# Eight pieces of w_ada: weighted sums on VectorE during the first layer's merge instead of thin matmuls on TensorE

## The chip, the cores and the metric

One core of one Trainium2 chip runs the whole program. The metric is the device time of one execution in microseconds (us). All data are float32.

## The reference, cut to what matters

Two layers of an attention, gated-linear-attention and gated-unit trunk (`trunk_layer`, 256 tokens and 256 context tokens, width 1024) are followed by two layers of a second kind. The change concerns the modulation vectors of the first two layers, and where in the first layer they are made:

```python
shift, scale, gate = jnp.split(jax.nn.silu(c) @ p['w_ada'] + p['b_ada'], 3, axis=-1)
shift_c, scale_c, gate_c = jnp.split(jax.nn.silu(c_ctx) @ p['w_ada'] + p['b_ada'], 3, axis=-1)
h = x * (1.0 + scale[:, None, :]) + shift[:, None, :]
...
m = (jax.nn.sigmoid(ga) * (ya @ p['w_br_attn'])
     + jax.nn.sigmoid(gg) * (yg @ p['w_br_gla'])
     + jax.nn.sigmoid(gs) * (ys @ p['w_br_sgu']))
return m @ p['w_out']
...
x_new = layer_norm(DEEPNORM_ALPHA * x + gate[:, None, :] * out, p['post_g'], p['post_b'])
```

`w_ada` is 1024 x 3072 for each layer: six pieces of 1024 x 512 a layer, twelve in all. Each piece is multiplied by two vectors, silu(c) and silu(c_ctx), which are the two columns of `cs3`. The first four pieces (shift and scale of layer 0, `ADA_FIRST`) are wanted at once. The other eight (`ADA_LATER`: the gate of layer 0 and all of layer 1) are wanted only behind the first layer's merge.

## The kernel before, in words

Each engine runs an instruction list of its own; semaphores order them (`Ev`; `Lane.wait_ge` waits).

**Weights.** SP loads all weight pieces in the order of `PLAN` into a ring of seven units of 1 MB. A piece of 1024 x 512 takes two units, a branch piece (512 x 512) one. Each load waits until the pieces that sat in its units are done with, and SP issues in order, so a load that waits holds back all behind it. `piece_done` says which event frees a piece.

**First layer, woven part** (41 to 395 us). TensorE, VectorE, ScalarE and GpSimd each run three generators, `dense`, `attention` and `gla`, one step at a time in an order written out by hand, `ORDER_A[0]`. Between the dense steps stand the eight later pieces of w_ada: a product step `ef` (`ada_products`: eight thin matmuls, each with two columns of `cs3` as the stationary side and 512 columns of weights as the moving side, and with its result at one of four row offsets of the bank), a copy on ScalarE (`ada_rows`), four transposes (`ada_columns`, `es`) and a short sum on VectorE (`ada_sum`).

**Merge of the first layer** (395 to 596 us). TensorE does the branch product of piece a0 (four groups of 128x512), then five pieces in the order g0, s0, a1, g1, s1 (`LATER`). Each of those has a gate part "m" and a branch part "b", and each part is made of seven half-size products (`WINOGRAD`, in the order 1, 2, 6, 7, 5, 4, 3). Products 6, 5 and 3 go to the bank of product 1, and 4 to that of 7, so each waits for ScalarE's copy of what the bank held. VectorE makes the sums over inputs (`input_sums`), adds the parts (`put`) and applies the gates (`gated`), in `later_piece`; GpSimd makes the sums over weights (`weight_sums`: four of 128x1024 for an "m" part, four of 128x512 for a "b" part) and adds the branches (four of 128x512 for each piece but a1). `gated` of pieces g and s writes the scratch tile `TM`, so each waits for GpSimd's add of the one before. After the merge come the gate rows (`gb`) and the product with w_out (`ou`).

Of the kernel before, what the change touches and what calls it, by code (L numbers as in the profile page):

```python
# [9 lines left out]
ALU = mybir.AluOpType  # L10
# [40 lines left out]
    "daadddddaddaddddadadgaaadgadgaadgdgaagdagadagadgadagadgagadgaadgadaaggadaaaggadggaadggagadgagdgaaddgaggadgggaa"  # L51
    "dgagdagdagdggadgdgaadgaagadagaagdadgaadgadagddaadaaaddaaadaagagadgaaaggagadgagagagadgadaggdaggggg",
# [9 lines left out]
def plan_a(l):  # L62
# [3 lines left out]
    if l == 0:  # L66
        for n, (m, j) in enumerate(ADA_LATER):
            out.insert(2 * n + 1, (f"a{m}ada{j}", 4096))
# [25 lines left out]
def dense_a(l):  # L94
# [3 lines left out]
    nth = [0]  # L98

    def ada():  # L100
        k = nth[0]
        nth[0] += 1
        if l:
            return []
        return ([("es", k - 1, "V")] if k else []) + ([("ef", k, "A")] if k < len(ADA_LATER) else [])

    q = [[("q", t, "A")] for t in tiles]
    kv = [[("kv", t, "A")] for t in range(4)]
    if l == 0:
        steps = q + [ada()] + kv + [[("lr", 0, "A")] + ada(), []]  # L110
    else:
        steps = kv[:2] + [[("hx", 0, "-")]] + kv[2:] + [[("lr", 0, "A")] + ada(), []] + q + [ada()]
    for name, kind in (("gqk", "A"), ("gv", "A"), ("ag", "T"), ("gg", "T"), ("su", "A"), ("sg", "T")):
        steps += [[(name, c, kind)] for c in range(4)] + [ada()]
    steps += [[("row", 0, "V")], [("bt", 0, "A")], [("sv", tiles[0], "A")], [("sv", tiles[1], "A")]]
    for t in tiles:
# [4 lines left out]
        else:  # L121
            steps += [[("mx", t, "V")] + ada()]
# [71 lines left out]
def build_program(nc, wf, consts, cT, xin, xinT, pa, ra, rpost, pb, rfin, out):  # L194
    with ExitStack() as ctx:
# [54 lines left out]
        par = ma.take(PA_SW)  # L250
        row = ma.take(640)
# [35 lines left out]
        HS = {n: r3(mw.take(1024), 4) for n in "1234"}  # L287
        E7 = SIGS.rearrange("p (a g n) -> p a g n", a=2, g=2)
# [83 lines left out]
        mg_sum = ev("mg_sum", 54)  # L372
        MS_T, MS_11, MS_22, MS_21, MS_B = 4, 8, 9, 10, 11
# [5 lines left out]
        FLAT[0] = FIRST + FLAT[0]  # L379
# [42 lines left out]
        MG_1, MG_11, MG_6, MG_7, MG_5, MG_22, MG_21, MG_12, MG_B = range(9)  # L422
# [60 lines left out]
        MGI = [{g: i for i, g in enumerate(x)} for x in MG]  # L483
        GATE = {g: i for i, g in enumerate(x for x in MG[1] if x[0] == "m")}
# [10 lines left out]
        for l in range(2):  # L495
# [3 lines left out]
            for i, g in enumerate(g for g in FLAT[l] if g[2] != "-" and (l, g[0]) != (0, "q")):  # L499
# [30 lines left out]
            seq = []  # L530
            for g in MG[l]:
                if l and g[0] == "m":
# [11 lines left out]
                seq.append((("mg", l) + g, freed))  # L544
            seq += [(("gb", l, i), gb_act.at(l, i)) for i in range(gb_pe.per[l])]
# [74 lines left out]
        def piece_done():  # L620
# [3 lines left out]
            for n, (l, j) in enumerate(ADA_LATER):  # L624
                out[f"a{l}ada{j}"] = dense_done(0, "ef", n)
# [56 lines left out]
        def merge_start(l):  # L682

            return [at_y.end(l), gl_y.end(l), gl_ms.end(l), gl_rs.end(l), dn_act.end(l), dn_dve.end(l), ys_done.end(l)]
# [67 lines left out]
        def _(e):  # L752
# [41 lines left out]
            def ada_columns(n, g, first):  # L794
                p.wait_ge(landed(d_id), dense_act(0, first, n))
                b = bank("dense", 0, g, n)
                for i in range(4):
                    ins = transpose(b, i, PT4[n % 2][:, 128 * i:128 * i + 128])
# [24 lines left out]
            def dense(l):  # L823
                L0 = l0(l)
                for step in DENSE[l]:
                    for n, i, kind in step:
                        if n == "ef":
                            ada_products(i, "ef", *ADA_LATER[i])
                            continue
                        if n == "es":  # L830
                            ada_columns(i, "es", "ef")
                            continue
# [189 lines left out]
            def layer_a(l):  # L1022
                L0 = l0(l)
                if l == 0:
                    for n in range(2):
                        ada_products(n, "pf", *ADA_FIRST[n])
                    for n in range(2):
                        ada_columns(n, "ps", "pf")
# [5 lines left out]
                    ada_columns(2, "ps", "pf")  # L1034
# [1654 lines left out]
```

## Time and profile before

| | |
|---|---|
| time, median of 3 runs | 1562.16 us (1559.05 to 1563.88) |
| the profiled execution: its own time | 1564.0 us |
| its span, first to last instruction | 1562.2 us |
| mean granted TensorE clock | 0.995 |

Read the shares of the engines first, then the chain that ended last, then the stages one by one: an engine's share of the whole span hides that the stages have different limits.

### The profile page before, as it was taken

Reading aid. Unit: us, or ns where it says so; the run is one execution under the profiler, and the core shown is the slowest. Engines: PE = TensorE matmul, PEld = TensorE weight load, DVE = VectorE, ACT = ScalarE, POOL = GpSimd, SP = SyncE. Lnnn points to the kernel's source line nnn. Section 1 sums busy time; section 2 is a strip of 40 time slices with the busy share of each in tenths; the row PEclk is TensorE's granted clock in tenths of the full one; section 3 lists DMA queues with packets and bytes.
Section 4 is the critical chain, followed back from the end, with each engine's and each line's share of the span. In section 5 each row is a group of like instructions: output and inputs, shape, how many; then the busy total and the mean of one; then the engine's idle time right before and its main releaser. Section 6 shows DMA issues by size and latency. Waiting matters only on the chain.

```text
span 1562.2 us, 19171 instructions
## 1 busy us (share of the span) xinstructions
PE 1516.4 (97%) x7888; PEld 1077.2 (69%) x7888; DVE 681.1 (44%) x1460; ACT 415.0 (27%) x814; POOL 281.9 (18%) x314
## 2 busy tenths in 40 slices
PE   6999999999999999999999999999999999999997
PEld 2544544455688885555877888588888758888873
DVE  1233433464633343523344311365687216568721
ACT  1122325232312210121235320134233213423320
POOL 0322210131455441113002102110100011010010
PEclk9999999999999999999999999999999999999999
DMA  8642222300122231322322243423221323332231
GB/s 362 262 175 108 108 108 108 135 27 17 65 81 81 97 123 68 150 108 97 119 108 108 102 156 120 175 102 144 109 110 71 147 115 149 126 112 106 88 128 40
DMA packets 17370, 184.22 MB, mean 118 GB/s; under 512 B 2306, under 2 KB 2818, under 8 KB 4740
## 3 DMA queue, kind: packets, MB, share of 16 engines
q1 hardware_dynamic: 17284, 183.01, 30.7%
q8 instruction: 62, 1.02, 0.3%
q14 instruction: 24, 0.20, 0.0%
HBM read 181.95 MB, written 1.05 MB: 117 GB/s over the span
## 4 chain that ended last, share of the span: by engine, by line
PE 89%; ACT 3%; DVE 3%; issue 2%; DMA 1%; POOL 1%; SPq 0%; POOLq 0%; ACTq 0%; DVEq 0%
PE ps L756 86%; PE ps L811 3%; DVE arena L1749 1%; DVE arena L1755 1%; DMA arena<-in_wf 1%; POOL arena L2362 1%; ACT arena L1333 1%; ACT L1709 0%; ACT L1707 0%; DVE arena L1752 0%; ACT arena L1577 0%; ACT arena L1707 0%; ACT arena L1593 0%; ACT L1595 0%; ACT L1593 0%
## 5 line engine op out<-in xcount | busy, mean ns | idle before, releaser
L756 PE MATMUL ps<-arena 128*128 128x256 f32 (+7 forms) x7396 | 1467.1, 383 | 33.8 <-DMA arena<-in_wf 12.3
L756 PEld LDWEIGHTS ps<-arena 128*128 128x128 f32 (+5 forms) x7396 | 1023.6, 178 | 445.4 <-issue 311.9
L2362 POOL TENSOR_TENSOR arena<-arena 128x256 f32<-128x256 f32 (+6 forms) x254 | 247.3, 994 | 825.8 <-DVE arena L1755 409.3
L1755 DVE SCALAR_TENSOR_TENSOR arena<-arena 128x256 f32<-128x256 f32 (+4 forms) x470 | 231.0, 545 | 143.4 <-ACT arena L1475 38.8
L1333 ACT ACTIVATE arena<-ps 128x512 f32<-128x512 f32 (+2 forms) x280 | 134.9, 505 | 448.3 <-PE ps L756 370.5
L1749 DVE TENSOR_TENSOR arena<-arena 128x512 f32<-128x512 f32 (+14 forms) x190 | 140.4, 761 | 170.9 <-ACT arena L1333 95.8
L1755 DVE SCALAR_TENSOR_TENSOR arena<-arena,ps 128x256 f32<-128x256 f32 (+2 forms) x121 | 54.0, 456 | 207.2 <-PE ps L756 96.9
L1749 DVE TENSOR_TENSOR arena<-ps,arena 128x512 f32<-128x512 f32 (+16 forms) x120 | 48.8, 434 | 106.0 <-PE ps L756 97.3
L811 PEld LDWEIGHTS ps<-arena 128*128 128x128 f32 x488 | 55.7, 141 | 29.4 <-issue 19.5
L811 PE MATMUL ps<-arena 128*128 128x128 f32 x488 | 71.5, 278 | 3.1 <-ACT arena L1611 1.5
L1752 DVE TENSOR_SCALAR arena<-arena 128x256 f32<-128x256 f32 (+9 forms) x181 | 62.8, 382 | 15.7 <-POOL arena L2362 10.8
L2366 POOL TENSOR_SCALAR arena<-arena 128x1 f32<-128x1 f32 (+2 forms) x22 | 16.2, 737 | 222.3 <-DVE arena L1802 79.2
L1755 DVE SCALAR_TENSOR_TENSOR arena<-ps,arena 128x128 f32<-128x128 f32 (+2 forms) x84 | 30.0, 407 | 59.3 <-PE ps L756 59.2
L1934 DVE COPY_PREDICATED arena<-arena,ps 128x512 f32<-128x512 uint32 (+1 forms) x56 | 30.1, 591 | 46.5 <-PE ps L756 46.5
L1559 ACT ACTIVATE arena<-ps,arena 128x256 f32<-128x256 f32 x32 | 14.9, 473 | 112.6 <-PE ps L756 107.3
L1372 ACT ACTIVATE arena<-ps 128x512 f32<-128x512 f32 (+1 forms) x24 | 11.8, 490 | 103.7 <-PE ps L756 103.7
L2535 POOL TENSOR_SCALAR arena<-arena 128x128 f32<-128x128 f32 x16 | 11.3, 726 | 110.7 <-DVE arena L1755 110.7
L1863 DVE TENSOR_REDUCE arena<-ps 128x1 f32<-128x512 f32 (+1 forms) x48 | 26.4, 590 | 9.6 <-PE ps L756 9.6
L1412 ACT ACTIVATE arena<-ps,arena 128x512 f32<-128x512 f32 (+1 forms) x48 | 29.0, 615 | 4.4 <-DVE arena L1752 4.4
L1381 ACT ACTIVATE arena<-ps 128x256 f32<-128x256 f32 (+1 forms) x24 | 10.1, 419 | 73.3 <-PE ps L756 73.3
L1455 ACT ACTIVATE arena<-arena 128x1024 f32<-128x1024 f32 (+1 forms) x28 | 23.3, 838 | 2.5 <-POOL arena L2362 2.5
L1563 ACT ACTIVATE arena<-ps 128x256 f32<-128x256 f32 x24 | 9.1, 380 | 54.7 <-PE ps L756 54.7
(96 smaller groups left out, 294.4 us busy)
## 6 DMA issues: line engine op xcount, KB each, us to landing
arena<-in_wf SPq DMA_DIRECT2D x69, 2048.0 KB, 8.3
arena<-in_wf SPq DMA_DIRECT2D x22, 1024.0 KB, 6.5
arena<-in_wf SPq DMA_DIRECT2D x2, 1152.0 KB, 7.7
arena<-in_xinT SPq DMA_DIRECT2D x2, 1024.0 KB, 15.9
arena<-in_xin SPq DMA_DIRECT2D x4, 512.0 KB, 3.9
arena<-in_rp SPq DMA_DIRECT2D x2, 1024.0 KB, 8.2
arena<-in_consts SPq DMA_DIRECT2D x1, 1410.0 KB, 21.6
arena<-in_pa SPq DMA_DIRECT2D x2, 532.0 KB, 9.4
```

Of the source, the lines that this page charges most:

```text
L756: return e.matmul(o, l, r, start=start, stop=stop, skip_group_check=True)
L811: return e.transpose(b[:, 128 * i:128 * i + rows], x, ident[0:rows, 0:rows])
L1333: return e.activation(o, i, ACT.Copy, **kw)
L1412: e.activation(Pb[h][:, 0:L], psum("att", l, "s", 2 * w + h)[:, 0:L], ACT.Exp, bias=sm[:, 1, h:h + 1], scale=0.125, accum_out=sm[:, 2, h:h ...
L1455: e.activation(x, x, ACT.Exp, scale=1.0 / 16).then_inc(gl_fe.hit(l, 7 * hp + n), 1)
L1749: return e.tensor_tensor(o, x, y, op)
L1752: return e.tensor_scalar(o, x, s1, None, op0) if s2 is None else e.tensor_scalar(o, x, s1, s2, op0, op1)
L1755: return e.scalar_tensor_tensor(out=o, in0=x, scalar=s, in1=y, op0=op0, op1=op1)
L1863: ins = e.reduce_max(sm[:, 0, h:h + 1], psum("att", l, "s", 2 * w + h)[:, 0:L], AX)
L1934: e.copy_predicated(att[:, tl[0]:4, h, :], both(2 ** n).unsqueeze(1).to_broadcast([128, nt, 128]), r3(psum("gla", l, "l", k)[:, L0:512], n ...
L2362: return e.tensor_tensor(o, x, y, op)
L2366: e.tensor_scalar(o, x, eps, None, ALU.add).then_inc(g.own(), 1)
```

## The change

The eight later pieces leave the woven part. Each is now made in the merge: VectorE adds up, over the eight chunks of 128 rows, weights times one number for each partition, once for silu(c) and once for silu(c_ctx): 16 instructions of 128x512 for a piece (`ada_later`). They are issued in quarters of four instructions, at places in the merge's VectorE list. TensorE then turns both sums (`et` and `es`, four transposes each) behind named products of the merge, and VectorE reduces them (`ada_turned`). `ORDER_A[0]` is a new string; the pieces stand elsewhere in the ring's order; ScalarE's tanh of the first quarter gate comes behind two copies instead of ahead of them.

```diff
+    if l == 0:
+        for (m, j), before in zip(ADA_LATER, ("ba0", "bg0", "ms0", "bs0", "ba1", "mg1", "bg1", "bs1")):
+            out.insert([n for n, _ in out].index("a0" + before), (f"a{m}ada{j}", 4096))
...
+        ACC = [[par_row[:, 0:512], par_row[:, 512:1024]], [par_row[:, 1024:1536], qkv_gv[:, 4608:5120]]]
+        BEHIND = [(*LATER[n], kind, x) for n, kind, x in ((0, "m", 7), (0, "b", 7), (1, "m", 5), (2, "m", 6), (2, "b", 7),
+                                                          (3, "m", 5), (4, "m", 6), (4, "b", 7))]
...
-                out[f"a{l}ada{j}"] = dense_done(0, "ef", n)
+                out[f"a{l}ada{j}"] = ada_acc.at(0, n)
...
 TensorE, behind each product of the merge
+                    for n, k, _ in turned_after(l, g):
+                        ada_columns(k, n, ACC[k % 2][n == "et"], ada_acc.at(0, k))
-                p.wait_ge(dense_dve(0, "es", 7))
+                p.wait_ge(dense_dve(0, "et", 7))
...
 ScalarE
-                    a.wait_ge(mg_dve.at(0, branch(*(LATER[n - 1] if n else ("a", 0)), 3)))
+                    a.wait_ge(mg_dve.at(0, branch(*LATER[n - 1], 3)) if n else None)
...
 VectorE
+            def ada_later():
+                for k, (l, j) in enumerate(ADA_LATER):
+                    w = weights(f"a{l}ada{j}", 8)
+                    made = [None, None]
+                    for kk in range(8):
+                        v.wait_ge(pieces[f"a{l}ada{j}"][2], dense_done(0, "et", k - 2) if k > 1 else None)
+                        for r in range(2):
+                            acc = ACC[k % 2][r]
+                            if kk == 0:
+                                ins = ts(acc, w[:, kk, :], cs3[:, kk, r:r + 1], None, ALU.mult)
+                            else:
+                                v.wait_ge(made[r])
+                                ins = stt(acc, w[:, kk, :], cs3[:, kk, r:r + 1], acc, ALU.mult, ALU.add)
...
+                        if kk % 2:
+                            yield
...
+                if n:
+                    next(quarters, None)
                 for kind, dst, o in (("m", SIG4, 0), ("b", BR, MS_B - MS_11)):
...
                     put(kind, 2, dst, 1, 1, MS_11 + o)
+                    if not o:
+                        turned("11")
+                        next(quarters, None)
+                        next(quarters, None)
...
                     tt(result(dst, 2, 2), E7, result(dst, 2, 2), ALU.add)
+                    if not o:
+                        turned("22")
+                        next(quarters, None)
                     if o:
                         gated(1, 2, 2, result(BR, 2, 2), mg_sum.at(0, 10 * n + MS_B + 1))
+                        turned("b22")
                     put(kind, 7, dst, 2, 1, MS_21 + o)
+                    if not o:
+                        next(quarters, None)
+                        next(quarters, None)
...
 VectorE, behind each of the four gate products of piece a0
+                            if l == 0:
+                                next(quarters)
```

The pieces are numbered k = 0 to 7 below; k is turned behind m7 of g0, b7 of g0, m5 of s0, m6 of a1, b7 of a1, m5 of g1, m6 of s1 and b7 of s1.

## Rows read from the trace of the kernel before

**Rows 1.** The page: shares of the engines, and the chain by engine.
```profile
PE 1516.4 (97%) x7888; PEld 1077.2 (69%) x7888; DVE 681.1 (44%) x1460; ACT 415.0 (27%) x814; POOL 281.9 (18%) x314
...
PE 89%; ACT 3%; DVE 3%; issue 2%; DMA 1%; POOL 1%; SPq 0%; POOLq 0%; ACTq 0%; DVEq 0%
```

**Rows 2.** Stages: length, busy us (count) of PE, PEld, DVE, ACT, POOL, granted clock.
```profile
41.00:395.00 354.00, 351.74 (x1519) 177.29 (x1520) 143.29 (x276) 110.14 (x216) 67.43 (x85) 1.00 0.31 120
...
402.40:424.30 21.90, 20.45 (x79) 14.56 (x77) 20.64 (x13) 1.76 (x4) 19.37 (x8) 1.00 0.00 1
424.30:446.80 22.50, 22.49 (x104) 19.85 (x105) 5.13 (x7) 5.28 (x9) 9.24 (x5) 1.00 0.25 94
446.80:591.90 145.10, 145.10 (x675) 127.78 (x673) 57.66 (x56) 28.71 (x48) 72.44 (x42) 1.00 0.24 88
```

**Rows 3.** Timeline of TensorE in short windows: dense products, thin products, transposes.
```profile
86.61 10.46 PE L756 MATMUL ps<-arena 128*128 128x512 f32 x24
...
106.04 1.90 PE L756 MATMUL ps<-arena 128*2 128x512 f32 x16
...
122.34 0.60 PE L811 MATMUL ps<-arena 128*128 128x128 f32 x4
```

**Rows 4.** Timeline of TensorE through the merge: start, length, count, idle before.
```profile
416.71 7.17 PE L756 MATMUL ps<-arena 128*128 128x256 f32 x32 [1.03 <-ACT arena L1333]
424.31 167.75 PE L756 MATMUL ps<-arena 128*128 128x256 f32 x776 [0.42 <-ACT arena L1333]
591.90 1.91 PE L811 MATMUL ps<-arena 128*128 128x128 f32 x16
596.34 56.78 PE L756 MATMUL ps<-arena 128*128 128x512 f32 x128 [2.53 <-issue]
```

**Rows 5.** Timeline of VectorE: start of the merge, end of g0, start of s0.
```profile
402.39 11.09 DVE L1749 TENSOR_TENSOR arena<-arena 128x1024 f32<-128x1024 f32 x4
413.40 2.47 DVE L1755 SCALAR_TENSOR_TENSOR arena<-arena,ps 128x512 f32<-128x512 f32 x4
...
447.10 2.82 DVE L1755 SCALAR_TENSOR_TENSOR arena<-arena 128x512 f32<-128x512 f32 x1 [0.78 <-POOL arena L2362]
451.31 0.69 DVE L1755 SCALAR_TENSOR_TENSOR arena<-arena,ps 128x512 f32<-128x512 f32 x1 [1.38 <-POOL arena L2362]
451.91 5.71 DVE L1749 TENSOR_TENSOR arena<-arena 128x512 f32<-128x512 f32 x4
457.54 0.68 DVE L1749 TENSOR_TENSOR arena<-ps,arena 128x512 f32<-128x512 f32 x1
```

**Rows 6.** Timeline of GpSimd in the same stretch.
```profile
402.43 19.53 POOL L2362 TENSOR_TENSOR arena<-arena 128x1024 f32<-128x1024 f32 x8 [39.27 <-DVE arena L1755]
...
445.80 3.58 POOL L2362 TENSOR_TENSOR arena<-arena 128x512 f32<-128x512 f32 x2 [1.85 <-DVE arena L1755]
...
452.07 8.03 POOL L2362 TENSOR_TENSOR arena<-arena 128x512 f32<-128x512 f32 x5 [0.80 <-DVE arena L1755]
471.34 4.67 POOL L2362 TENSOR_TENSOR arena<-arena 128x1024 f32<-128x1024 f32 x2 [11.24 <-PE ps L756]
```

**Rows 7.** Timeline of VectorE in the third layer: a chain of weighted sums.
```profile
1060.27 3.25 DVE L1755 SCALAR_TENSOR_TENSOR arena<-arena 128x256 f32<-128x256 f32 x8
```

**Rows 8.** Groups of VectorE by shape, whole span: count, busy us, mean ns.
```profile
L1752 DVE TENSOR_SCALAR arena<-arena 128x512 f32<-128x512 f32 x40 | 20.5, 545 | 11.3 <-POOL arena L2362 10.8
...
L1863 DVE TENSOR_REDUCE arena<-ps 128x1 f32<-128x512 f32 x32 | 20.4, 678 | 5.7 <-PE ps L756 5.7
```

**Rows 9.** The same view in steps of 1 us, behind TensorE's wait before w_out.
```profile
598.00:599.00 1.00, 1.00 (x2) 0.34 (x1) 0.00 (x0) 0.00 (x0) 0.00 (x0) 0.50 0.79 242
599.00:600.00 1.00, 1.00 (x3) 0.53 (x2) 0.00 (x0) 0.00 (x0) 0.00 (x0) 0.70 1.00 328
```

**Rows 10.** DMA issues of weights: KB each, median us from issue to landing.
```profile
arena<-in_wf SPq DMA_DIRECT2D x69, 2048.0 KB, 8.3
arena<-in_wf SPq DMA_DIRECT2D x22, 1024.0 KB, 6.5
```

More of the change, by code:

```diff
@@ L249, in build_program @@
         GK, GQ = GKQ[:, :, 0, :], GKQ[:, :, 1, :]
-        par = ma.take(PA_SW)
-        row = ma.take(640)
+        par_row = ma.take(PA_SW + 640)
+        par, row = par_row[:, 0:PA_SW], par_row[:, PA_SW:PA_SW + 640]
         tv = ma.take(2048)
@@ L378, in build_program @@
                  ("ps", 2, "V"), ("qh", 3, "-"), ("ps", 3, "V")]
-        FLAT[0] = FIRST + FLAT[0]
+        TURNED = [("e" + "st"[r], k, "V") for k in range(8) for r in range(2)]
+        FLAT[0] = FIRST + FLAT[0] + TURNED
         GROUP = [{g[:2]: i for i, g in enumerate(f)} for f in FLAT]
@@ L498, in build_program @@
                     hold(("ht", s, kp), 3 + i % 5, (ht_dve if s else ht_act).at(1, 2 * kp + 1))
-            for i, g in enumerate(g for g in FLAT[l] if g[2] != "-" and (l, g[0]) != (0, "q")):
+            for i, g in enumerate(g for g in FLAT[l] if g[2] != "-" and (l, g[0]) != (0, "q") and g not in TURNED):
                 hold(("dense", l) + g[:2], i % 2, (dense_act if g[2] == "A" else dense_dve)(l, *g[:2]))
@@ L529, in build_program @@
                 hold(("gla", l, n, k), 5 + i % 3, by.at(l, k))
-            seq = []
+            seq, extra = [], []
             for g in MG[l]:
+                seq += extra
+                extra = [(("dense", 0, n, k), dense_dve(0, n, k)) for n, k, _ in turned_after(l, g)]
                 if l and g[0] == "m":
@@ L1766, in ada_sum, with ada_turned @@
                     ).then_inc(dn_dve.hit(0, BY_DVE[0][(g, n)]), 1)
+            def ada_later():
[11 more added lines that the diff above has]
+                                ins = stt(acc, w[:, kk, :], cs3[:, kk, r:r + 1], acc, ALU.mult, ALU.add)
+                            if (kk, r) == (7, 1):
+                                ins.then_inc(ada_acc.hit(0, k), 1)
+                            else:
+                                ins.then_inc(v.own(), 1)
+                                made[r] = v.now()
+                        if kk % 2:
+                            yield
+            def ada_turned(k):
+                l, j = ADA_LATER[k]
+                for r, g in enumerate(("es", "et")):
+                    v.wait_ge(dense_done(0, g, k), landed(d_bada, l))
+                    a4 = AS[:, 4 * r:4 * r + 4]
+                    e.tensor_reduce(a4, r3(psum("dense", 0, g, k), 4), AX, ALU.add).then_inc(v.own(), 1)
+                    v.wait_ge(v.now())
+                    stt(r3(SCOL[l], 24)[:, 4 * j:4 * j + 4, r], a4, 1.0 if j in (2, 3) else 0.0,
+                        BADA[:, 24 * l + 4 * j:24 * l + 4 * j + 4], ALU.add, ALU.add
+                        ).then_inc(dn_dve.hit(0, BY_DVE[0][(g, k)]), 1)
+                    v.wait_ge(dense_dve(0, g, k))
             def dense(l):
@@ L1984, in later_piece, with turned @@
                 input_sums(HB, {"a": AG, "g": GG, "s": SG}[br], 10 * n + MS_T)
+                def turned(place):
+                    for k, at in enumerate(((0, "22"), (0, "b22"), (1, "22"), (2, "22"), (2, "b22"), (3, "22"), (4, "22"),
+                                            (4, "b22"))):
+                        if at == (n, place):
+                            ada_turned(k)
+                if n:
+                    next(quarters, None)
                 for kind, dst, o in (("m", SIG4, 0), ("b", BR, MS_B - MS_11)):
@@ L2019, in layer_a @@
                     input_sums(HS, hT, 0)
+                    quarters = ada_later()
                 for j in range(2):
```

87 lines of the change are left out of this document (35 added, 52 removed).

## The prediction

> **What bounds the kernel now.** The page comes first: TensorE is busy for 97% of the span, and the chain that ended last is TensorE for 89% [rows 1]. So a change pays only as far as it takes time from TensorE's list, and costs as far as it makes TensorE wait. The windows by stage say where there is room: in the woven part TensorE is busy 351.7 of 354.0 us, in the last four merge pieces 145.1 of 145.1, while VectorE is busy 57.7 of those 145.1 [rows 2]. The timeline of TensorE shows the merge's waits: 1.0 and 0.4 us in piece g0, 2.5 us ahead of w_out, nothing between [rows 4]. VectorE's and GpSimd's timelines show what the shares hide: how long their instructions take when both run [rows 5, 6].
>
> **What the woven part gives back.** A thin product is 16 records of TensorE. Dense records of 512 columns come every 0.43 us (24 in 10.46), but the 16 thin ones take 1.90 together, since they run beside one another [rows 3]. I count 1.8 for a piece, the last record's tail lying under the next product: 8 x 1.8 = 14.4 us, not 8 x 6.9 = 55. Four transposes pass in 0.60 with their tail, 16 in 1.91 [rows 3, 4]: 0.11 each, 0.44 a piece, 3.5 for eight. Removed: 17.9 us. ScalarE's copies and VectorE's small sums go too; both engines are mostly idle there (110 and 143 of 354 busy [rows 2]), so they count nothing. The new order string keeps TensorE's other work. It could at best remove the 2.3 us of idle time, and could bring waits, since 17.9 us of filler are gone between the same chains; I count 0, and 0 to +5 for the range. In it the last GLA product stands alone behind the last dense group, not in a pair, so I let VectorE enter the merge 5.3 us behind TensorE's first merge product. Before it was 7.4: that product began at 395.0 (416.7 less the 1.0 wait, less 32 records at 0.43 and 32 at 0.216), and VectorE began at 402.4 [rows 4, 5].
>
> **What the merge takes on, without waits.** TensorE: 8 x 2 x 4 = 64 transposes at 0.11 = +7.0. VectorE: 16 multiplies at 0.5 [rows 8] and 112 weighted sums. A chain of weighted sums of 128x512 is not in the trace. Four independent ones with one input from PSUM take 2.47, 0.61 apart, and one alone lasts 0.69 [rows 5]; in the chain of 256 columns eight take 3.25, 0.40 apart [rows 7], so chained ones follow each other almost, but not quite, end to end, which for 512 columns I put at 0.67. Bounds 0.61 and 0.67; I take the middle, 0.64. That is 72 + 8 = 80 us, and 16 reductions at 0.68 with a small sum each, 0.9 in all, make 14. VectorE's idle time in the merge is 1.3 + 17.4 + 87.4 = 106 us [rows 2]. So 94 of 106 us would be filled before any wait is counted.
>
> **What they wait for.** With GpSimd working, VectorE's instructions with two SBUF inputs stretch: four of 128x1024 take 11.09 us beside GpSimd's sums, four of 128x512 take 5.71 though one takes 0.69 alone, and one gate takes 2.82 while GpSimd finishes a sum; the one that reads PSUM keeps its 0.68 [rows 5, 6]. GpSimd stretches too (4.67 for two of 1024 alone, 19.53 for four of 1024 and four of 512 beside VectorE; 8.03 for five of 512 against 1.27 for one). The numbers fit turns taken one whole instruction at a time: 1.15 + 2.2 us for a pair of 1024, 0.6 + 1.15 for a pair of 512. All 128 new instructions are of the kind that waits. A rule of the Trainium skill says the same (SBUF — State Buffer, section Who interferes with whom): a VectorE instruction with two SBUF inputs and a GpSimd one that reads SBUF exclude each other for the whole instruction. By that rule the idle 106 us aren't free for sums, and it speaks against the change. The trace agrees with it (5.71 against 4 x 0.6).
>
> **The wait that TensorE gets.** Each turning stands in TensorE's list and waits for its accumulation; all products behind it wait too. I walked the merge, instruction by instruction, with those durations, with turns between VectorE and GpSimd, and 8.3 and 6.5 us for a load [rows 10]. The same walk of the kernel before puts the start of w_out 201.4 us behind the first merge product; the rows have 596.3 - 395.0 = 201.3 [rows 4]. One step in full, piece s0, from TensorE's first product on: the gates of g0 end 6 us in (446.8 against 452.0 now [rows 5], and a turning more), input sums with GpSimd beside 5.7, a quarter 2.7, `put` 0.7, two quarters 5.3, and about 2 more for the rest of GpSimd's sums: 22 to 23. TensorE has its five "m" products done at 5 x 3.45 = 17.3. So it waits 5 to 6 us for k = 2. Likewise, each at 0.61 and at 0.67 a sum:
> - k = 0, behind m7 of g0: 2.5 and 3.4 (VectorE does 11.1 us of input sums, four gates and 16 sums, TensorE needs 27.6);
> - b6 of g0: 3.3 and 4.5. It needs ScalarE's copy of b1, in whose list the tanh of a `put` stands, and that `put` now has three quarters and a reduction ahead of it;
> - m6 of s0: 2.5 and 3.5 (ScalarE's first copy waits for the last gate of g0);
> - k = 2: 5.3 and 6.0; k = 5, behind m5 of g1: 3.9 and 4.6;
> - k = 3 and k = 6, behind m6 of a1 and s1: 2.0 and 2.3 each. There only the input sums and one quarter fit in 10.4 us, of which 5 are gone with the gates before;
> - m6 of a1, g1, s1: 1.5 and 2.7 together.
>
> Sum 23.0 and 29.3; middle 26.2. The two waits in g0 now go in it (in the walk 2.5 us with their like), because ScalarE no longer waits for VectorE there: -2.5. Ahead of w_out the wait grows by 1.3, as the last reduction (1.8) stands before three gates. So the merge: 7.0 + 26.2 - 2.5 + 1.3 = +32.0, 28.9 and 34.9 at the bounds.
>
> The ring: bg0 sits where piece 0 sat, so its load waits for the accumulation, 6.5 us before GpSimd's next sums; ba1 and bs1 wait for k = 3 and 6 alike, mg1 and ms1 for the piece before and k = 5. In the walk each lands before TensorE needs it, and what is late is GpSimd, whose sums fall onto VectorE's quarters; that is in the sum. Behind the merge, w_out's second half waits for k = 7 and lands about when it is needed: 0, and 3 for the range.
>
> TensorE's clock: behind the 2.5 us wait it runs at half speed to about 599.6, some 3.3 us, a loss of 1.7 [rows 9]. Five of the waits are as long. But TensorE then waits for VectorE again, which was not slowed, so most of it is swallowed: I count 0, and up to 5 x 1.7 = 8.5 for the range.
>
> **The sum.** -17.9 + 32.0 = +14.1 us. On the profiled span 1562.2 that is 1576.3, its own time 1564.0 giving 1578.1; on the median 1562.16, 1576.3. Bounds of this case: 28.9 - 17.9 = +11 and 34.9 - 17.9 + 5 + 3 + 4 = +29, thus 1573 to 1591.
>
> **The rivals.**
> - *The sums fit in* (faster). VectorE and GpSimd hardly meet, and TensorE sees only its own list: -17.9 + 7.0 - 2.5 + 1.3 and the one wait that a walk without turns leaves (2.2, m6 of s0) = -9.9, 1552. For it: 106 us of idle time for 94 us of work. Against it: the 5.71 and 2.82 rows, and in piece a1 even that idle time lies behind the product that waits. It decides at the sum of waits: below 17.9 - 7.0 + 2.5 - 1.3 = 12 us the change pays. Chance 0.17.
> - *Half the waits* (about the same). If the quarters mostly slip past GpSimd, the waits at k = 2, 3, 5, 6 that a chain without turns still has, 1 to 4 us each, leave some 12 us: +0, 1562. Chance 0.11.
> - *VectorE and GpSimd bound the merge* (slower still). If a sum costs 0.8 us, the walk gives waits of 43 us and +49 for the merge, +31 with the woven part: 1593; clock losses that aren't swallowed lead to the same place. For it: turns cost more than a pair's sum in the first rows (3.3 us a pair of 1024). Chance 0.14.
> - My forecast: 0.58.
>
> **Range and chances.** The likeliest case has 1573 to 1591. The range that leaves out no more than 2 in 10 takes in the faster side too: 1551 to 1592. A measurement of this kernel tells about 0.3% (5 us) from no change. Faster by more than that: 0.18 (the first rival and a bit of the second); within: 0.11; slower: 0.71.
>
> **What would show it.** In the woven part TensorE's busy time falls by 18 us, and by its other waits it is seen whether the new order holds. In the merge, VectorE's weighted sums show single durations well over 0.69 where GpSimd runs; TensorE's waits are released by VectorE ahead of transposes (k = 2, 5, 3, 6, in that order of length) and by ScalarE ahead of b6 of g0; the granted clock drops behind them. VectorE is busy for over 85% of the merge. The prediction is wrong if the weighted sums keep 0.6 us beside GpSimd, if a sum costs nearer 0.4, or if VectorE is far enough ahead that TensorE finds each accumulation done.

## Result: 1578.1 us, and the profile after

The changed kernel takes 1578.08 us (median, 1576.53 to 1581.74) beside 1561.66 of the kernel before on the same chip (1559.05 to 1563.88): ratio 1.0109, 95% interval [1.0085, 1.0133]. It is slower. Predicted were 1576.3, in 1551 to 1592, with 0.71 for slower. The profiled execution has 1581.74 as its own time, the longest of the four, and a span of 1579.9.

The page after, shares and chain [rows 1 before]:

```profile
PE 1514.2 (96%) x7792; PEld 1081.3 (68%) x7792; DVE 789.9 (50%) x1604; ACT 410.1 (26%) x806; POOL 285.2 (18%) x314
...
PE 60%; DVE 8%; ACT 3%; issue 2%; POOL 2%; DMA 0%; POOLq 0%; ACTq 0%; DVEq 0%
```

TensorE's busy time hardly moved, 1516.4 to 1514.2. VectorE has 109 us more, and its share of the chain went from 3% to 8%. The page alone says "still TensorE": the changed kernel's chain has 60% of TensorE where it had 89%. The windows say where it broke (length, busy of PE, PEld, DVE, ACT, POOL, then the clock; the woven part, the merge up to w_out, the rest) [rows 2]:

```profile
41.00:373.60 332.60, 332.40 (x1359) 171.24 (x1360) 141.77 (x262) 108.58 (x210) 66.20 (x85) 1.00 0.20 75
373.60:611.90 238.30, 212.99 (x953) 177.56 (x951) 198.04 (x240) 40.20 (x67) 108.22 (x56) 0.97 0.36 140
611.90:1579.90 968.00, 941.39 (x5370) 723.28 (x5370) 444.81 (x1084) 255.66 (x520) 109.33 (x168) 0.99 0.31 115
```

The first merge product starts at 373.65 (the row that holds it ends at 401.25; less 32 records at 0.43 and 64 at 0.216). Before it was 395.0, so the woven part gave back **21.35 us**. The product with w_out starts at 611.95, before at 596.34: the merge takes 238.3 for 201.3, **+37.0 us**. Together +15.6 at w_out.

In the timelines below, L762 is TensorE's products, L817 its transposes, L1753 VectorE's weighted sums and gates, L1747 its sums of two tensors, L1750 its multiplies, L2416 GpSimd's sums and L1335 ScalarE's copies. TensorE through the merge: start, length, count, idle before and its releaser [rows 4]:

```profile
403.09 1.09 PE L817 MATMUL ps<-arena 128*128 128x128 f32 x8 [1.84 <-DVE arena L1753]
422.37 6.59 PE L762 MATMUL ps<-arena 128*128 128x256 f32 x16 [4.38 <-ACT arena L1335]
443.25 10.63 PE L762 MATMUL ps<-arena 128*128 128x256 f32 x48 [1.32 <-ACT arena L1335]
458.83 1.91 PE L817 MATMUL ps<-arena 128*128 128x128 f32 x8 [4.96 <-DVE arena L1753]
488.29 3.72 PE L762 MATMUL ps<-arena 128*128 128x256 f32 x16 [0.79 <-ACT arena L1335]
493.79 1.10 PE L817 MATMUL ps<-arena 128*128 128x128 f32 x8 [1.78 <-DVE arena L1753]
530.18 10.63 PE L762 MATMUL ps<-arena 128*128 128x256 f32 x48 [1.61 <-ACT arena L1335]
543.13 1.09 PE L817 MATMUL ps<-arena 128*128 128x128 f32 x8 [2.33 <-DVE arena L1753]
572.60 3.72 PE L762 MATMUL ps<-arena 128*128 128x256 f32 x16 [0.79 <-ACT arena L1335]
578.11 1.09 PE L817 MATMUL ps<-arena 128*128 128x128 f32 x8 [1.78 <-DVE arena L1753]
607.03 1.52 PE L817 MATMUL ps<-arena 128*128 128x128 f32 x12 [1.05 <-DVE arena L1753]
610.61 0.65 PE L817 MATMUL ps<-arena 128*128 128x128 f32 x4 [2.06 <-DVE arena L1753]
611.95 8.40 PE L762 MATMUL ps<-arena 128*128 128x512 f32 x15 [0.69 <-POOL arena L2416]
```

Each x8 row of transposes (L817) with a wait is one turned piece: k = 0, 2, 3, 5, 6. Each L762 row that waits for ScalarE's copy (L1335) is a product 6. The waits ahead of w_out's rows belong to the last piece. Look at 458.83: the same eight transposes that take 1.09 elsewhere take 1.91 behind the longest wait. The windows of 2 us there give the reason, the granted clock (last but two):

```profile
458.00:460.00 2.00, 1.17 (x6) 1.17 (x7) 1.46 (x4) 0.59 (x1) 0.00 (x0) 0.73 0.50 90
460.00:462.00 2.00, 2.00 (x8) 1.73 (x7) 1.86 (x5) 0.04 (x1) 0.00 (x0) 0.50 0.64 229
462.00:464.00 2.00, 2.00 (x10) 1.73 (x9) 1.97 (x4) 0.00 (x0) 0.00 (x0) 0.91 0.98 418
```

After 4.96 us without work the clock is at 0.50, the level of 1.2 GHz, to about 462.

VectorE's timeline shows what its sums cost, alone and beside GpSimd [rows 5]:

```profile
393.81 2.73 DVE L1753 SCALAR_TENSOR_TENSOR arena<-arena 128x512 f32<-128x512 f32 x4
...
406.87 8.11 DVE L1753 SCALAR_TENSOR_TENSOR arena<-arena 128x512 f32<-128x512 f32 x6
...
416.22 0.16 DVE L1753 SCALAR_TENSOR_TENSOR arena<-arena 128x4 f32<-128x4 f32 x1
...
437.42 1.55 DVE L1753 SCALAR_TENSOR_TENSOR arena<-arena 128x4 f32<-128x4 f32 x1
...
442.48 5.72 DVE L1747 TENSOR_TENSOR arena<-arena 128x512 f32<-128x512 f32 x4
448.12 4.76 DVE L1753 SCALAR_TENSOR_TENSOR arena<-arena 128x512 f32<-128x512 f32 x4
...
453.40 5.38 DVE L1753 SCALAR_TENSOR_TENSOR arena<-arena 128x512 f32<-128x512 f32 x8
...
465.70 9.58 DVE L1753 SCALAR_TENSOR_TENSOR arena<-arena 128x512 f32<-128x512 f32 x8
```

GpSimd's timeline in the same stretch [rows 6]:

```profile
407.92 6.52 POOL L2416 TENSOR_TENSOR arena<-arena 128x512 f32<-128x512 f32 x4 [16.64 <-DMA arena<-in_wf]
...
442.64 8.36 POOL L2416 TENSOR_TENSOR arena<-arena 128x512 f32<-128x512 f32 x5 [0.80 <-DVE arena L1753]
468.65 5.41 POOL L2416 TENSOR_TENSOR arena<-arena 128x1024 f32<-128x1024 f32 x2 [17.65 <-PE ps L762]
```

Between 451.0 and 468.6 GpSimd is still, and eight sums take 5.38, 0.66 apart. Across GpSimd's pairs eight take 9.58, and six take 8.11. The 4-column sum (0.16) becomes 1.55: it starts at 437.42, in the middle of a GpSimd sum of 128x1024 that runs from 436.60 to 438.95, and ends at 438.97. The chain of 512 columns that the trace of before didn't have is thus 2.73 for four, 0.66 apart: the upper of my two bounds.

The rest is not the change's. Behind the start of w_out the profiled execution takes 968.0, before 965.9, and in the runs below, whose code from there on is the same but for the PSUM banks in three of them, 960.8 to 965.9. I put the 2 us down to the scatter of one profile.

### The profile page after: what moved, and what is told of

The parts are those of the page before. It is cut to its first block, busy times and chain, and to the rows that moved or that the text cites. A ratio compares the mean times of both kernels' runs of the same rounds, so it can differ in the third digit from the quotient of the medians.

```text
span 1579.9 us, 19120 instructions
## 1 busy us (share of the span) xinstructions
PE 1514.2 (96%) x7792; PEld 1081.3 (68%) x7792; DVE 789.9 (50%) x1604; ACT 410.1 (26%) x806; POOL 285.2 (18%) x314
## 3 DMA queue, kind: packets, MB, share of 16 engines
HBM read 181.95 MB, written 1.05 MB: 116 GB/s over the span
## 4 chain that ended last, share of the span: by engine, by line
PE 60%; DVE 8%; ACT 3%; issue 2%; POOL 2%; DMA 0%; POOLq 0%; ACTq 0%; DVEq 0%
PE ps L762 58%; DVE arena L1753 5%; DVE arena L1747 3%; PE ps L817 2%; POOL arena L2416 2%; ACT arena L1335 1%; DVE arena L1750 0%; ACT L1707 0%; ACT L1705 0%; DMA arena<-in_wf 0%; DVE arena L1792 0%; ACT arena L1575 0%; ACT arena L1705 0%; ACT arena L1591 0%; ACT L1593 0%
## 5 line engine op out<-in xcount | busy, mean ns | idle before, releaser
L762 PE MATMUL ps<-arena 128*128 128x256 f32 (+10 forms) x7268 | 1461.6, 382 | 37.6 <-ACT arena L1335 12.0
L762 PEld LDWEIGHTS ps<-arena 128*128 128x128 f32 (+5 forms) x7268 | 1023.0, 180 | 438.9 <-issue 296.8
L1753 DVE SCALAR_TENSOR_TENSOR arena<-arena 128x256 f32<-128x256 f32 (+4 forms) x590 | 333.3, 619 | 153.6 <-ACT arena L1473 46.1
L2416 POOL TENSOR_TENSOR arena<-arena 128x256 f32<-128x256 f32 (+6 forms) x254 | 250.6, 1008 | 851.5 <-DVE arena L1753 412.6
L1335 ACT ACTIVATE arena<-ps 128x512 f32<-128x512 f32 (+3 forms) x272 | 130.1, 502 | 470.6 <-PE ps L762 396.3
L1747 DVE TENSOR_TENSOR arena<-arena 128x512 f32<-128x512 f32 (+14 forms) x190 | 131.5, 715 | 120.3 <-ACT arena L1335 42.9
L1753 DVE SCALAR_TENSOR_TENSOR arena<-arena,ps 128x256 f32<-128x256 f32 (+2 forms) x121 | 54.3, 456 | 204.2 <-PE ps L762 98.4
L817 PE MATMUL ps<-arena 128*128 128x128 f32 x520 | 76.9, 280 | 18.2 <-DVE arena L1753 15.8
L817 PEld LDWEIGHTS ps<-arena 128*128 128x128 f32 x520 | 60.5, 142 | 48.7 <-issue 21.6
L1747 DVE TENSOR_TENSOR arena<-ps,arena 128x512 f32<-128x512 f32 (+16 forms) x120 | 48.6, 434 | 67.6 <-PE ps L762 58.8
L1750 DVE TENSOR_SCALAR arena<-arena 128x256 f32<-128x256 f32 (+8 forms) x197 | 71.4, 398 | 15.8 <-POOL arena L2416 10.8
L1753 DVE SCALAR_TENSOR_TENSOR arena<-ps,arena 128x128 f32<-128x128 f32 (+2 forms) x84 | 30.1, 407 | 69.3 <-PE ps L762 69.2
```

Of the source, the lines that this page charges most:

```text
L762: return e.matmul(o, l, r, start=start, stop=stop, skip_group_check=True)
L817: return e.transpose(b[:, 128 * i:128 * i + rows], x, ident[0:rows, 0:rows])
L1335: return e.activation(o, i, ACT.Copy, **kw)
L1747: return e.tensor_tensor(o, x, y, op)
L1750: return e.tensor_scalar(o, x, s1, None, op0) if s2 is None else e.tensor_scalar(o, x, s1, s2, op0, op1)
L1753: return e.scalar_tensor_tensor(out=o, in0=x, scalar=s, in1=y, op0=op0, op1=op1)
```

## The experiments

All are made from the changed kernel unless it is said. "Merge" is from the first merge product to w_out's start in each profile. The last transposes of the woven part stand at 363.30 in the changed kernel, 10.35 ahead of the first merge product; I take the same 10.35 in each run. "Walk" is what the hand walk gives for that kernel, as in the expectations. They take 0.66 us for a sum, so the changed kernel's walk is 235 and not the 233.3 (201.3 + 32.0) of the prediction. The 209 of "PSUM, second places" counts lost clock too; the 234 below it doesn't and stands beside 207.

| run | median us (before beside it) | ratio, 95% | merge | walk |
|---|---|---|---|---|
| the kernel before | | | 201.3 | 201.4 |
| the changed kernel | 1578.08 (1561.66) | 1.0109 [1.0085, 1.0133] | 238.3 | 235 |
| small weight sums | 1548.93 (1561.08) | 0.992 [0.9898, 0.9941] | 208.1 | 208 |
| running sums in PSUM | 1568.76 (1561.08) | 1.0051 [1.0033, 1.0069] | 231.3 | 223 |
| other places | 1558.6 (1561.08) | 0.9989 [0.9976, 1.0003] | 221.8 | 217 |
| PSUM and places | 1556.11 (1561.08) | 0.9966 [0.9953, 0.9979] | 219.6 | 211 |
| few sums | 1558.38 (1561.27) | 0.9983 [0.9971, 0.9996] | 219.1 | 212 |
| resident data | 1588.72 (1561.27) | 1.0184 [1.0167, 1.0201] | 252.2 | 243 |
| left out | 1540.16 (1561.27) | 0.9866 [0.9851, 0.988] | 199.4 | |
| sums in the woven part | 1606.64 (1561.27) | 1.0299 [1.0281, 1.0317] | | |
| PSUM, second places | **1545.54** (1558.84) | **0.9912** [0.9899, 0.9926] | 208.8 | 209 |
| second places, SBUF | 1571.71 (1559.68) | 1.0073 [1.0056, 1.009] | 233.0 | 234 |
| before, ScalarE's order | 1557.84 (1558.84) | 0.9988 [0.9979, 0.9997] | | |

**Take GpSimd's share away.** The theory was turns between VectorE and GpSimd; the rival, a chain of sums too long by itself.

```diff
-                    w11, w12, w21, w22 = (quarter(w, k, f) for f, k in ("11", "12", "21", "22"))
+                    w11, w12, w21, w22 = (quarter(w, k, f)[:, :, 0:16] for f, k in ("11", "12", "21", "22"))
+                    o = {x: y[:, :, 0:16] for x, y in o.items()}
```

> The changed kernel, with GpSimd's weight sums of the five later pieces cut to 16 of their 256 columns (the rest of WS and WB keeps old numbers); everything waits for everything as before, and VectorE's 128 new instructions stay. Theory of turns (VectorE's sums with two SBUF inputs and GpSimd's sums take turns): nearly all waits go, w_out starts about 27 us earlier in the merge, 1548 to 1553 us, VectorE's sums come 0.66 us apart nearly everywhere and their mean falls from 0.94 to about 0.70 us. Rival, the chain of sums alone is too long for the places where it is turned: VectorE's sums were the bound by their number, so the time stays within 5 us of 1578. Rival, GpSimd late with the weight sums themselves: also faster, but VectorE's mean of a sum would not fall.

1548.9, within the range on record. The changed kernel's merge stands 31.9 us above 199.4 + 7.0 (the merge without the pieces, from the run that leaves them out, and the 64 transposes); here 30.2 of them go, though VectorE has all its sums. VectorE's group of sums in that merge (count, busy, mean ns):

```profile
L1753 DVE SCALAR_TENSOR_TENSOR arena<-arena 128x512 f32<-128x512 f32 x129 | 88.3, 738 | 6.1 <-ACT arena L1473 3.3 <-POOL arena L2416 1.6
```

In the changed kernel the same 129 have a mean of 940 ns. The rival falls: the number of sums isn't what TensorE waits for. The second rival, GpSimd late by itself, asked for a mean that doesn't fall; as GpSimd is also done sooner here, it is the PSUM pair below that leaves its work as it was.

**Take VectorE's share away.**

```diff
+                            if (kk, r) not in ((0, 0), (7, 1)):
+                                continue
-                            if kk == 0:
+                            if (kk, r) in ((0, 0), (7, 1)):
```

> The changed kernel with 14 of the 16 sum instructions of each piece left out (one chunk's product stands for the sum of eight); loads, turnings, reductions, places and GpSimd's sums stay. Theory of turns: the waits come from the product of the two engines' work, so taking VectorE's share away gives as much as taking GpSimd's did: by the walk 212 us from the first merge product to w_out for 235, thus 1555, 1551 to 1559. Rival, the turnings and the small sums behind them cost, wherever VectorE stands: 1565 or more.

1558.4, within the range on record but 3 us over its centre. One wait of 6.1 us is new: ScalarE's first copy of s0 waits for the last gate of g0, and GpSimd's wide sums, which had waited 17.7 us for a load, fell on just those gates (one gate waits 3.5 us and lasts 2.8). Each engine's share taken away gives 20 to 29 us, which together is more than the 31.9 there are: the cost is in their meeting. The rival asked for 1565 or more.

**Is it the ring?** The sums read hT, which is in SBUF, and the pieces aren't loaded.

```diff
-        for (m, j), before in zip(ADA_LATER, ("ba0", "bg0", "ms0", "bs0", "ba1", "mg1", "bg1", "bs1")):
-            out.insert([n for n, _ in out].index("a0" + before), (f"a{m}ada{j}", 4096))
...
-                    w = weights(f"a{l}ada{j}", 8)
+                    w = hT
```

> The changed kernel, but the sums read the layer's input hT, which lies in SBUF, with a constant as the factor; the eight pieces are not loaded at all and hold nothing of the ring. Same instructions, same places. Theory of turns: loads don't set the waits, the time stays at 1578, or grows by up to 8 us, since GpSimd's weight sums then come earlier and fall on the a0 stage's first sums. Rival, the ring (pieces that sit in it until their sums are done hold back the loads of the branch pieces, GpSimd starts late): the time falls by 5 us or more, to 1573 or less.

1588.7, over 10 us slower (8 at most were expected), so the range on record was missed; the rival asked for a gain. A freer ring makes it worse: GpSimd's first sums, which had waited 16.6 us for a load between the wide and the narrow ones, now follow without a break, and VectorE's first sums of a quarter stretch (two multiplies 3.39 for 2.38, the two sums behind them 3.42 for 1.40):

```profile
377.76 19.44 POOL L2413 TENSOR_TENSOR arena<-arena 128x1024 f32<-128x1024 f32 x8 [43.93 <-DVE arena L1750]
```

The first turning then waits 5.3 us for 1.8. More of the loss comes later: k = 3 and k = 6 wait 5.94 us each, where the changed kernel waits 1.78. GpSimd's narrow sums for a1 follow there at once (five instructions from 487.14 on, 8.34 us), where they had waited 9.26 us for a load, and the input sums beside them take 5.71 for 3.56. The late loads were a help.

**Leave the pieces out,** loads, sums, turnings and all (a constant stands for their vectors).

> The changed kernel without the eight later pieces: no load, sum, turning or reduction of them (the vectors they make are a constant). It shows the two halves of the sum apart: the woven part as changed, and the merge without its new work. From the changed kernel's trace the woven part gave back 21 us, and ScalarE's new order should save the 2.5 us of waits in piece g0: 1562 - 21 - 2.5 = 1538, 1534 to 1542. If the woven part's 21 us came from the ring rather than from TensorE's list, the trace shows it by a shorter woven part still (over 1 us less than in the changed kernel). Rival, ScalarE's order gives nothing: the merge up to w_out stays at 201 us.

1540.2, and w_out's product starts at

```profile
573.03 55.17 PE L747 MATMUL ps<-arena 128*128 128x512 f32 x128 [2.54 <-issue]
```

The woven part ends where it ended in the changed kernel, so its 21.35 us don't hang on the loads of the pieces. The merge takes 199.4, 1.9 less than before: that is ScalarE's order. In one sum: what the change moved to the merge costs 238.3 - 199.4 = 38.9 us there.

**ScalarE's order alone,** in the kernel before.

```diff
-        MG_1, MG_11, MG_6, MG_7, MG_5, MG_22, MG_21, MG_12, MG_B = range(9)
+        MG_1, MG_6, MG_7, MG_11, MG_5, MG_22, MG_21, MG_12, MG_B = range(9)
```

> The kernel before with only ScalarE's part of the change: the tanh of the first quarter gate behind the copies of products 6 and 7, and the wait for piece a0's last gate moved to the copies that write its tile. The two waits of TensorE in piece g0 (1.0 and 0.4 us) go, and the time with them: 1560, 1558 to 1562. Rival, nothing: 1561 to 1562, the waits stay or others take their place. In neither case does it explain more than 2.5 of the change's microseconds.

w_out's product starts at 594.00 for 596.34, the two waits in g0 are gone, and 1557.84 stands beside 1558.84, 0.1% less, with an interval that just leaves out no change: 0.5 to 3 us. The change's effect is of that size or nearly: the expectation named 2.5 as the most.

**The running sum in PSUM.** A weighted sum then has one SBUF input; the last writes SBUF.

```diff
+                hold(("acc", r), 6 + r, ada_acc.at(0, 7))
...
-                            acc = ACC[k % 2][r]
+                            acc, o = psum("acc", r), ACC[k % 2][r] if kk == 7 else psum("acc", r)
```

> The changed kernel, the two running sums of a piece kept in two PSUM banks (only the last of the eight sums writes SBUF), so that each weighted sum has one SBUF input and one from PSUM; the merge's other banks rotate over six instead of eight. Same places, same work. Theory of turns, in which an instruction with one SBUF input doesn't take turns with GpSimd: sums keep 0.66 us beside GpSimd, and by the walk of the merge with these numbers 12 us go: 1566, 1561 to 1570. Rival, the chain's length and not the turns: 1578 or, as a bank's rotation is tighter, slower. Rival, any SBUF input takes turns: unchanged within 3 us.

**Other places** for quarters, turnings and loads, same instructions.

> The changed kernel, same instructions, other places: most turnings stand later in TensorE's list and the quarters of sums stand where the walk of the merge finds the fewest waits (three quarters ahead of the input sums of pieces a1 and g1, none in the a0 stage but two), the pieces of w_ada one or two places earlier in the ring. Theory of turns by the walk: 217 us from the first merge product to w_out instead of 235, thus 1560, 1556 to 1568. Rival, VectorE and GpSimd are already the bound of the merge (their busy time and turns fill it): places can't help, 1573 to 1582.

**Both,** with places of its own:

> Running sums in PSUM and places chosen for that case. Theory of turns by the walk: 211 us from the first merge product to w_out, thus 1554, 1549 to 1560; if the sums don't take turns and nothing else comes in, it beats the kernel before (1562). Rival, the chain's length or the tighter rotation of banks: 1565 or more.

1568.8, 1558.6 and 1556.1, all in their ranges. "Any SBUF input takes turns" and "VectorE and GpSimd are the bound, places can't help" both fall: places alone give 20 us. The last is the first version with all of its work that is faster than the kernel before. Both PSUM runs stood 8 to 9 us above their walk in the merge. In the first of them the two longest waits of TensorE are these:

```profile
439.39 15.70 PE L764 MATMUL ps<-arena 128*128 128x256 f32 x64 [4.61 <-DVE arena L1755]
522.53 16.78 PE L764 MATMUL ps<-arena 128*128 128x256 f32 x64 [5.09 <-DVE arena L1755]
```

They stand ahead of m2 of s0 and of g1. With a rotation over six banks m2 takes the bank of product b1 of the piece before, which the last gate frees; with eight it takes one that has long been free. The changed kernel waits 1.32 and 1.61 us there, one product later. Without the bank wait m6 could start 0.69 us behind the last gate, as it does there; with it m2 starts at the gate's end and takes 3.45 first. So I estimate that the tighter rotation, which the expectation named in a rival, took back 2 x 2.8 = 5.6 us of what PSUM gave at these places. I had put the 8 to 9 us down to two other things that the walk lacked: the 128x4 sums, which take turns too (0.16 or 1.55, above), and lost clock, and chose the places anew with both in the walk ("p" and "s" are ahead of and behind a piece's input sums, "11" to "b22" the places behind its `put` and gate steps):

```diff
-        BEHIND = [(*LATER[n], kind, x) for n, kind, x in ((0, "m", 7), (0, "b", 7), (1, "m", 5), (2, "m", 6), (2, "b", 7),
-                                                          (3, "m", 5), (4, "m", 6), (4, "b", 7))]
+        BEHIND = [(*LATER[n], kind, x) for n, kind, x in (
+            (0, "m", 7), (1, "m", 3), (2, "m", 2), (2, "b", 1), (3, "m", 2), (4, "m", 2), (4, "m", 3), (4, "b", 6))]
...
+            QUARTERS = [{'21': 2, 's': 1, '22': 1},
+                        {'11': 3, 'b11': 1, 'b22': 1},
+                        {'11': 2, 'p': 1, '21': 2, '22': 1},
+                        {'21': 1, 'p': 5, 'b22': 1, '22': 1},
+                        {'11': 4, '22': 1}]
...
+                    for k, at in enumerate(((0, "b11"), (1, "21"), (2, "p"), (2, "b11"), (3, "b11"), (4, "21"), (4, "b11"), (4, "b11"))):
...
+                            for _ in range((1, 2, 1, 0)[c] if l == 0 else 0):
```

> As the run with running sums in PSUM and chosen places, the places chosen anew after that run: the walk now also counts 1.5 us of lost clock for each wait over 1.9 us and 0.68 to 0.70 us for the first multiply into PSUM, and finds 209 us from the first merge product to w_out (the run before measured 219.7 where the same walk gives 214 and one clock loss more). Theory of turns: 1549, 1546 to 1554, three waits of TensorE at most that are over 1 us. Rival, the 5 to 6 us by which both PSUM runs were above their walk come from the tighter banks or from PSUM itself: 1553 to 1557, no better than before.

1545.5, 0.9912 [0.9899, 0.9926]: **faster than both kernels,** by 13 us and by some 31 (0.9912 to 1.0109), and 0.5 us below its range of 1546 to 1554. The merge takes 208.8, 2.4 above the 199.4 + 7.0 of one in which TensorE waits for nothing new. Its window:

```profile
373.60:582.20 208.60, 204.94 (x952) 173.88 (x951) 174.68 (x240) 39.75 (x66) 98.34 (x56) 1.00 0.42 159
```

**The same places, the sum in SBUF.** Two kernels that differ in where the running sum lies, in what that brings with it (six banks or eight), and in the place of one wait of VectorE's for `et`, which ends no wait of its sums in either trace.

> The places of the fastest run (the second set, 1545.5), but the running sums in SBUF as in the changed kernel, eight banks again. The two differ only in where the running sum lies. Theory of turns: by the walk 234 us from the first merge product to w_out against 207, six waits of TensorE over 2 us come back, 1545.5 + 26 = 1572, 1566 to 1578. Rival, the gain of that run came from its places and not from PSUM: 1545 to 1555.

1571.7, where 1572 was expected. Each works alone, places by 20 us and PSUM by 9 against the changed kernel, but neither alone is clearly faster than the kernel before (0.9989 and 1.0051); these places, made for PSUM, cost 26 us with the sums in SBUF. The same stretch of the two, VectorE and GpSimd, first with PSUM:

```profile
390.58 5.35 DVE L1755 SCALAR_TENSOR_TENSOR ps<-arena,ps 128x512 f32<-128x512 f32 x8
...
392.11 5.08 POOL L2423 TENSOR_TENSOR arena<-arena 128x512 f32<-128x512 f32 x4 [0.61 <-DMA arena<-in_wf]
```

and with SBUF:

```profile
388.07 4.47 DVE L1750 TENSOR_SCALAR arena<-arena 128x512 f32<-128x512 f32 x2
...
395.40 7.82 DVE L1753 SCALAR_TENSOR_TENSOR arena<-arena 128x512 f32<-128x512 f32 x8
...
392.79 6.59 POOL L2420 TENSOR_TENSOR arena<-arena 128x512 f32<-128x512 f32 x4 [0.52 <-DMA arena<-in_wf]
```

With PSUM eight sums run from 390.58 to 395.93, beside GpSimd's from 392.11 on, and both keep their pace: 0.66 and 1.27 apiece. With SBUF both stretch, and two multiplies take 4.47. The waits come back to TensorE, five of over 2 us where six were expected. Three of them:

```profile
406.53 1.97 PE L817 MATMUL ps<-arena 128*128 128x128 f32 x8 [4.77 <-DVE arena L1753]
...
523.46 1.97 PE L817 MATMUL ps<-arena 128*128 128x128 f32 x8 [4.07 <-DVE arena L1753]
...
567.07 17.53 PE L762 MATMUL ps<-arena 128*128 128x256 f32 x80 [2.99 <-ACT arena L1335]
```

The Trainium skill (SBUF — State Buffer, section Who interferes with whom) states the other half of the rule that the prediction cited: a VectorE instruction with at most one SBUF input, outside the two-port modes, doesn't contend with GpSimd. The 5.35 and 5.08 agree. The condition may matter here: the multiplies have one SBUF input as well, and from SBUF to SBUF two of them take 4.47 beside GpSimd's wide sums, where into PSUM two take 1.40 (at 387.36 in the fastest run, GpSimd's wide sums running to 391.49). In which mode they ran no trace shows.

**A place where GpSimd is idle,** the woven part, in the order string of the kernel before: a miss.

```diff
+    for k in range(0 if l else 8):
+        steps[(9, 13, 18, 23, 28, 33, 38, 43)[k]].insert(0, ("es", k, "V"))
+        steps[(11, 15, 20, 25, 30, 35, 40, 46)[k]].insert(0, ("et", k, "V"))
+        for i in ((4, 5, 6, 7), (8, 9, 10, 11), (13, 14, 15, 16), ..., (38, 39, 40, 41))[k]:
+            steps[i].append(("eq", k, "-"))
```

> The same sums on VectorE, turned and reduced in the same way, but in the woven part in the order string of the kernel before, not in the merge: quarters behind the dense steps of the first layer, the turnings of a piece one dense piece later, running sums in four tiles that are free there. GpSimd is busy 67 us of 354 there, not 104 of 201. Theory of turns (the place is what costs): thin products gone 14.4, 32 transposes more +3.5, ScalarE's order in the merge -2.5, so 1562 - 13 = 1549, 1544 to 1556. Rival, a quarter of 2.7 us on VectorE delays the attention's and the gated-linear chain's own steps wherever it stands: TensorE waits in the woven part, 1562 or more.

1606.6, where 1549 was expected: the slowest of all, and the rival's case. The last transposes of the woven part stand at 427.62, before at 387.31, 40.3 us later; the merge is 2.0 us shorter. TensorE's waits from 41 to 410 us: total, times, longest:

```profile
PE ps L812 <- DVE arena L1751: 10.0, 2, 9.4
PE ps L757 <- DVE arena L1751: 5.7, 2, 3.3
PE ps L757 <- DVE arena L1968: 5.5, 2, 2.9
PE ps L812 <- DVE arena L1745: 3.9, 2, 3.0
PE ps L757 <- DMA arena<-in_wf: 3.7, 1, 3.7
```

The first turning comes 9.4 us too early, the dense piece behind waits 3.7 for its load, and the gated-linear chain's own VectorE steps (L1968) are late behind quarters. The granted clock is 0.94 over the stretch from 41 to 411. "Idle" in a window of 354 us was no room: VectorE's steps there lie inside chains that TensorE follows closely. How much of it better places would save, I haven't tried.

## Why the prediction was right

The forecast's case came, and for its reason: TensorE waits for sums that take turns with GpSimd, at the places that the walk had named. The total is nearer than its parts, and that is luck. Forecast were -17.9 + 32.0 = +14.1 us, measured up to w_out -21.35 + 37.0 = +15.6. The merge lies above its own 28.9 to 34.9 (the terms as printed add up to 28.8 and 35.1); slower matmuls, counted as 0, cost 9 us more, while the waits came out 4.6 and the woven part 3.45 below the forecast. Point by point, by its steps:

- **Woven part, -17.9: measured -21.35.** Thin products and transposes came out 1.4 us too small (busy 351.74 to 332.40 is 19.3), and "new order 0" was 2.1 too low: the 2.3 us of idle time fell to 0.2. That is what I allowed the order at best; whether it is the order's doing or that of the steps gone was not tested apart.
- **Transposes 7.0:** eight take 1.04 to 1.10 with their tail, less what overlaps; right as far as the rows tell.
- **Waits, 26.2: measured 21.6** (the first ten of the timeline), below the range of 23.0 to 29.3. The list held, in the order k = 2, 5, then 3 and 6: k0 1.8 (2.5 to 3.4), b6 of g0 4.4 (3.3 to 4.5), m6 of s0 1.3 (2.5 to 3.5), k2 5.0 (5.3 to 6.0), k3 and k6 1.8 each (2.0 to 2.3), k5 2.3 (3.9 to 4.6), m6 of a1, g1, s1 3.2 together (1.5 to 2.7). VectorE's input sums began 4.3 us behind the first merge product (377.98), not 5.3, which helped k0.
- **Ahead of w_out +1.3:** 1.05 + 2.06 + 0.69 for 2.53, +1.3. **ScalarE's order -2.5:** -1.9.
- **The clock, 0 with up to 8.5: the mis-sized term.** 238.3 less 199.4, 7.0 and the waits beyond those that the kernel without the pieces has (25.4 - 2.5) leaves 9.1 us. It can be read another way: TensorE is busy 213.0 us in the merge, before 197.4 and 7.0 are due for transposes, so 8.6 more for the same work. In the run with second places in SBUF the same sum leaves 9.1 again (waits 20.0), in the fastest run, with one wait over 2 us, 1.3. Not all of it is the clock. In the changed kernel's merge the granted clock is low in three stretches, 421.3 to 428.3 (0.51), 458.8 to 462.4 (0.53) and 544.2 to 547.8 (0.53), at the end of the waits of 4.38, 4.96 and 2.33 and behind them, and 1.00 elsewhere; I estimate from these that it cost some 6.3 us, and in the run with second places in SBUF some 7. In the fastest run it is 1.00 all through the merge and 1.3 remain. The rest I put down to TensorE's start behind each of the thirteen waits (16 records behind one take 3.72, in an unbroken row 16 x 0.216 = 3.45). I had argued that the loss is swallowed, since TensorE waits for VectorE again. That the waits came out 4.6 us smaller than forecast fits half of it being swallowed, but no run shows that this is why. The 9 should have been in the sum.
- **Ring, 0:** no wait of TensorE for a load, and without the ring it is slower, as measured.
- **Turn-taking:** shown by three pairs: GpSimd's share away (1549), VectorE's share away (1558), PSUM for SBUF at the same places (1546 and 1572). It was the step on which the case rested. "All 128 new instructions are of the kind that waits" held too, though 16 of them, the multiplies, have one SBUF input: they average 0.57 us, and 0.48 with GpSimd's sums cut short.
- VectorE is busy for 83% of the merge, not "over 85%"; its 129 sums of 512 columns (a few of them gates) average 0.94 us, where without turns they average 0.74.

The rivals: "The sums fit in" needed waits under 12 us; they were 21.6 with clock lost besides. With PSUM they are 1.1, and there it came true, at 1546 for its 1552. "VectorE and GpSimd bound the merge" asked for 0.8 us a sum; 0.66 it is alone, and the stretch beside GpSimd is in the walk already. The 3.3 us for a pair of 1024, which the prediction named for it as more than the pair's sum, is that sum (1.15 + 2.2 = 3.35).

Open: the 9 us by which the resident-data run's merge lies above its walk, and 7 us of the few-sums run's, are put down to lost clock and to the place of GpSimd's sums from their timelines, not tested apart. The resident-data run's merge is also read from the longest of its four executions. The walk with the two additions meets the fastest run within 1 us; for the PSUM run before it, it gives 214 and a clock loss more where 219.6 were measured, so some 4 us stay unexplained there, and the walk of the first PSUM run lacks the bank waits above. The 234 for the SBUF run leaves the clock out, so its 233.0 holds waits that were smaller than the walk's.

## What to carry to other kernels

Idle time of VectorE is room for an instruction with two SBUF inputs (here also for a multiply from SBUF to SBUF) only where GpSimd is idle too; count a pair as the sum of both. Put the running value of such a chain in PSUM and both engines keep their pace: here 26 us between two kernels at the same places. The banks that it takes can bring waits of their own (4.61 and 5.09 us at the first places). Before work is moved behind a place in TensorE's list, walk the list with the durations beside one another: the walk found the waits, in order, and later the places that, with the sums in PSUM, turned 16 us lost into 13 won. And where TensorE waits over 2 us several times, count slower matmuls behind: 9.1 us over the five of the run with second places in SBUF, 1.8 each. It is a mean: there the clock fell behind three of the five, and behind those of 2.14 and 2.99 it didn't.

## What the runs showed of the hardware

- Chained weighted sums of 128x512 follow each other 0.66 us apart, in SBUF (4 in 2.73) and with the running value in PSUM (8 in 5.35). The first multiply costs 0.44 into SBUF when free, 0.70 into PSUM (a pair in 0.88 and 1.40).
- The turn was taken by instructions of every size measured: the sum of 128x4 lasts 0.16 alone and 1.55 when GpSimd is in the middle of an instruction, and ends within 0.02 us of it. Reductions from PSUM keep 0.69 in every run.
- A multiply by a number for each partition, with one SBUF input and its result in SBUF, took turns too: two in 0.87 alone, in 2.38 and 4.47 beside GpSimd. With the result in PSUM two took 1.40 beside GpSimd.
- A load that comes late can make a kernel faster: with the ring out of play GpSimd's sums came earlier and the merge of the profiled execution took 14 us more (the median 10.6).
